# Hybrid decoder block on one core: the first norm's scale by its own transfer, the parameter transposes later, half of group 0 from split parts

## What is computed

```python
u = rms_norm(h, norm1_g)
proj = u @ w_in                      # 1024 x 4608
y_conv = conformer_conv(proj[..., :1024], ...)       # a * sigmoid(g), 31-tap depthwise conv, layer norm, silu, @ w_conv_out
y_attn = attention(q, k, v) @ w_attn_out             # 8 heads of 64, from the next 1536 columns
g = sigmoid(proj[..., 2560:] + b_gates)
h = h + (g[..., :1024] * y_conv + g[..., 1024:] * y_attn) @ w_out
h = h + moe_ffn(rms_norm(h, norm2_g), ...)           # top 4 of 32 experts, clamped SwiGLU, 1024 wide
```

## Time and profile before

| | |
|---|---|
| median of 3 runs | 1130.43 us (1129.95 to 1130.46) |
| the profiled execution | 1127.98 us |
| its span, first to last instruction | 1126.2 us |
| TensorE busy | 967.3 us (86%) |
| VectorE busy | 393.8 us (35%) |
| ScalarE busy | 309.8 us (28%) |
| mean granted clock of TensorE | 0.938 |
| moved by DMA | 432.97 MB, mean 384 GB/s |

### The profile page before, as it was taken

The page is one execution under the profiler, slowest core; times in us unless marked ns, Lnnn a source line. Parts: engine busy times, 40 slices in busy tenths (PEclk is TensorE's granted clock), DMA queues, the critical chain, the costliest instruction groups (busy, mean ns, idle before and its releaser), DMA issues.

```text
span 1126.2 us, 19760 instructions
## 1 busy us (share of the span) xinstructions
PE 967.3 (86%) x7261; PEld 445.8 (40%) x7262; DVE 393.8 (35%) x1014; ACT 309.8 (28%) x534; POOL 5.3 (0%) x27
## 2 busy tenths in 40 slices
PE   6999899998666769899996799998996976998667
PEld 5998689632211213233331233332332321332112
DVE  4699966432111112223232133322322321232111
ACT  4565573222111111212221122221221211222111
POOL 1000000000000000000000000000000000000000
PEclk8999999999888898999998899998999998999887
DMA  7473259999999999999999999999999999999996
GB/s 270 169 290 122 103 182 402 387 414 425 425 427 426 427 428 426 427 425 426 427 427 425 428 425 426 425 428 425 426 425 427 427 426 427 426 427 429 425 427 250
DMA packets 50918, 432.97 MB, mean 384 GB/s; under 512 B 4845, under 2 KB 5265, under 8 KB 18128
## 3 DMA queue, kind: packets, MB, share of 16 engines
q1 hardware_dynamic: 50424, 432.50, 92.3%
q10 hardware_dynamic: 472, 0.16, 0.1%
HBM read 431.59 MB, written 1.05 MB: 384 GB/s over the span
## 4 chain that ended last, share of the span: by engine, by line
PE 48%; DMA 24%; SPq 20%; DVE 4%; issue 2%; ACT 1%; DVEq 0%; ACTq 0%
PE bank L1312 16%; SPq L404 12%; DMA up_odd<-in_w_up_gate 10%; DMA up_even<-in_w_up_gate 10%; PE bank L1043 9%; PE bank L1346 8%; SPq L410 6%; PE bank L1234 5%; DMA down_even<-in_w_down 3%; PE bank L1303 3%; PE bank L1281 2%; DVE up_odd L723 2%; PE bank L1073 1%; PE bank L1332 1%; DVE w_lo L698 1%
## 5 line engine op out<-in xcount | busy, mean ns | idle before, releaser
L1312 PE MATMUL bank<-up_even,reg_r 128*32 128x512 f32 x1472 | 189.9, 661 | 68.2 <-DMA up_even<-in_w_up_gate 68.2
L1312 PE MATMUL bank<-up_odd,reg_r 128*32 128x512 f32 x1408 | 179.4, 654 | 66.1 <-DMA up_odd<-in_w_up_gate 66.1
L998 DVE TENSOR_TENSOR ys<-reg_m,ys 64x512 fp32r<-64x512 f32 x90 | 61.7, 685 | 236.6 <-ACT ys L650 236.0
L1312 PEld LDWEIGHTS bank<-up_even,reg_r 128*32 128x32 f32 x1472 | 47.0, 115 | 203.6 <-DMA up_even<-in_w_up_gate 103.9
L1312 PEld LDWEIGHTS bank<-up_odd,reg_r 128*32 128x32 f32 x1408 | 44.9, 115 | 194.0 <-DMA up_odd<-in_w_up_gate 99.1
L638 ACT ACTIVATE reg_m<-reg_m 128x256 f32<-128x256 f32 x45 | 18.9, 420 | 370.4 <-DVE reg_m L979 370.4
L1234 PE MATMUL bank<-reg_h,reg_r 128*32 128x256 f32 x736 | 93.2, 636 | 0.7 <-DVE reg_r L869 0.7
L979 DVE TENSOR_SCALAR reg_m<-bank 128x256 f32<-128x256 f32 x45 | 19.1, 425 | 211.7 <-PE bank L1312 211.7
L646 ACT ACTIVATE reg_m<-bank,gslot 128x512 f32<-128x512 f32 x45 | 30.9, 688 | 195.5 <-PE bank L1346 195.5
L1346 PE MATMUL bank<-down_even,reg_r 128*32 128x512 f32 x736 | 84.4, 596 | 0.4
L1346 PE MATMUL bank<-down_odd,reg_r 128*32 128x512 f32 x704 | 80.7, 596 | 0.5 <-DMA down_odd<-in_w_down 0.5
(11 more groups left out here) (252 smaller groups left out, 1188.1 us busy)
## 6 DMA issues: line engine op xcount, KB each, us to landing
up_even<-in_w_up_gate SPq DMA_DIRECT2D x64, 2048.0 KB, 35.8
up_odd<-in_w_up_gate SPq DMA_DIRECT2D x64, 2048.0 KB, 38.5
down_even<-in_w_down SPq DMA_DIRECT2D x64, 1024.0 KB, 36.5
down_odd<-in_w_down SPq DMA_DIRECT2D x64, 1024.0 KB, 36.5
down_even<-in_w_in SPq DMA_DIRECT2D x6, 2048.0 KB, 8.4
down_odd<-in_w_in SPq DMA_DIRECT2D x2, 2048.0 KB, 8.7
down_odd<-in_w_in SPq DMA_DIRECT2D x4, 512.0 KB, 8.5
down_odd<-in_w_attn_out SPq DMA_DIRECT2D x1, 2048.0 KB, 8.0
```

Of the source, the lines that this page charges most:

```text
L998: ins = nc.vector.tensor_tensor(ys[64:P, half, :], YR[r, :], ys[0:64, half, :].bitcast(F32), ALU.subtract)
L1312: ins = mm(UP[q * SLOTS:(q + 1) * SLOTS, :], XT[:, k % 2, k // 2 * SLOTS:(k // 2 + 1) * SLOTS], up_columns(a, k, q), start=False, stop=(k ...
```

## The change

The change does four things. `norm1_g` goes by a transfer of its own straight into a new tile `g1c` (128 partitions of 8 values), with its own semaphore `g1_in`; `par` shrinks from 38 to 30 rows, and the multiplies that make uT wait for `g1_in` and not for the parameters. The four parameter transfers of SP are issued behind group 0's, and their transposes on TensorE and copies on VectorE stand later. To fit the order of the scale's transfer, feature p*8+k now lies at partition p, step k: the transposes of x read every eighth column (`features(m)`), and `w_in` is read by `(p k)`, not `(k p)`. Half of group 0 (its columns 256 to 511) is split and computed as the other groups are.

```diff
-        par = sb("par", [P, 38])
+        par = sb("par", [P, 30])
+        g1c = sb("g1c", [P, KD])
...
-        win = w_in.rearrange("(k p) n -> p k n", p=P)
+        win = w_in.rearrange("(p k) n -> p k n", k=KD)
...
SP:
-            sp.dma_start(dwr, conv_dw).then_inc(par_in, 16)
-            sp.dma_start(rows[8:24, :], b_gates...).then_inc(par_in, 16)
-            for r, src in ((36, q_norm_g), (37, k_norm_g)):
-                sp.dma_start(rows[r:r + 1, :]..., src...).then_inc(par_in, 16)
...
                 if i == 0:
                     for c in range(4):
                         sp.dma_start(dst[:, 2 * c:2 * c + 2, :], src[:, 2 * c:2 * c + 2, :]).then_inc(g0_in[c], 16)
+                    sp.dma_start(dwr, conv_dw).then_inc(par_in, 16)
+                    sp.dma_start(rows[0:16, :], b_gates...).then_inc(par_in, 16)
+                    for r, src in ((28, q_norm_g), (29, k_norm_g)):
+                        sp.dma_start(rows[r:r + 1, :]..., src...).then_inc(par_in, 16)
ScalarE:
-            for r, src, n in ((0, norm1_g, 8), (24, conv_dw_b, 4), (28, conv_ln_g, 4), (32, conv_ln_b, 4)):
+            act.dma_start(g1c[:], norm1_g.rearrange("(p k) -> p k", k=KD)).then_inc(g1_in, 16)
+            for r, src, n in ((16, conv_dw_b, 4), (20, conv_ln_g, 4), (24, conv_ln_b, 4)):
                 act.dma_start(rows[r:r + n, :], src.rearrange("(r c) -> r c", c=P)).then_inc(par_in, 16)
...
             def weights_high(i, b):
-                arrived(act, i)
+                if i == 0:
+                    for c in range(4):
+                        act.wait_ge(g0_in[c], 16)
+                else:
+                    arrived(act, i)
...
+            weights_high(0, 1)
             for b in range(2):
                 weights_high(1, b)
VectorE:
-            dve.wait_ge(par_full, 1)
-            nc.vector.tensor_copy(par[:], PAR_BANK[:, 0:38]).then_inc(par_ready, 1)
-            nc.vector.tensor_copy(dwT[:], PAR_BANK[:, 64:...]...).then_inc(par_ready, 1)
             dve.wait_ge(ssx, 1)
             nc.vector.reciprocal(st[:, 4:6], st[:, 2:4]).then_inc(rstd_ready, 1)
-            dve.wait_ge(par_ready, 2)
+            dve.wait_ge(g1_in, 16)
...
-                dve.wait_ge(w_hi_ready, 2 * (i - 1) + b + 1)
+                dve.wait_ge(w_hi_ready, 2 * i + b)
...
-            for i in (1, 2):
-                for b in range(2):
-                    weights_low(i, b)
+            weights_low(0, 1)
+            for b in range(2):
+                weights_low(1, b)
+            dve.wait_ge(par_full, 1)
+            nc.vector.tensor_copy(par[:], PAR_BANK[:, 0:30]).then_inc(par_ready, 1)
+            nc.vector.tensor_copy(dwT[:], PAR_BANK[:, 64:...]...).then_inc(par_ready, 1)
+            for b in range(2):
+                weights_low(2, b)
+            dve.wait_ge(par_ready, 2)
TensorE:
-                        ins = nc.tensor.transpose(bank[...][:, c:c + P], hx[:, m, k * P:(k + 1) * P], ident[:])
+                        ins = nc.tensor.transpose(bank[...][:, c:c + P], features(m)[:, k, :], ident[:])
...
-            pe.wait_ge(par_in, 16 * 9)
-            (the five transposes of rows and dwr, before the rstd products)
...
-            for b in range(2):          # both halves of group 0 in full precision
+            claim(U_G)                  # the first half in full precision, as before
...
+            pe.wait_ge(par_in, 16 * 8)
+            (the five transposes of rows and dwr)
             pe.wait_ge(u_lo_ready, 1)
+            channel_group_bank(0, 1)    # waits for w_lo_ready, then 48 split matmuls
             for b in range(2):
                 channel_group_bank(1, b)
```

More of the change, by code:

```diff
@@ L136, in features @@
             return hx[:, m, :].rearrange("t (f k) -> t k f", k=KD)
-        rows = REG_R[0:38, 512:640]
+        rows = REG_R[0:30, 512:640]
         dwr = REG_R[0:TAPS, 0:512]
@@ L204, in hybrid_block @@
         hotT = sb("hotT", [P, MT, P], F32R)
-        g1c, bgc = par[:, 0:8], par[:, 8:24]
-        dwb, lng, lnb = par[:, 24:28], par[:, 28:32], par[:, 32:36]
-        qg, kg = par[:, 36:37], par[:, 37:38]
+        bgc = par[:, 0:16]
+        dwb, lng, lnb = par[:, 16:20], par[:, 20:24], par[:, 24:28]
+        qg, kg = par[:, 28:29], par[:, 29:30]
         bank = [ctx.enter_context(nc.psum_tensor(f"bank{i}", [P, 512], F32)) for i in range(8)]
@@ L360, in _ @@
                         sp.dma_start(dst[:, 2 * c:2 * c + 2, :], src[:, 2 * c:2 * c + 2, :]).then_inc(g0_in[c], 16)
+                    sp.dma_start(dwr, conv_dw).then_inc(par_in, 16)
+                    sp.dma_start(rows[0:16, :], b_gates.rearrange("(r c) -> r c", c=P)).then_inc(par_in, 16)
+                    for r, src in ((28, q_norm_g), (29, k_norm_g)):
+                        sp.dma_start(rows[r:r + 1, :].rearrange("r (h d) -> r h d", h=2),
+                                     src.rearrange("(r h d) -> r h d", r=1, h=1).to_broadcast([1, 2, HD])).then_inc(par_in, 16)
                 else:
@@ L1024, in _ @@
                         c = k % 2 * T + m * P
-                        ins = nc.tensor.transpose(bank[(U_XT + b) % 4][:, c:c + P], hx[:, m, k * P:(k + 1) * P], ident[:])
+                        ins = nc.tensor.transpose(bank[(U_XT + b) % 4][:, c:c + P], features(m)[:, k, :], ident[:])
                     if m == MT - 1:
                         ins.then_inc(bank_full[(U_XT + b) % 4], 1)
-            pe.wait_ge(par_in, 16 * 9)
[L1029 to L1032, removed]
             pe.wait_ge(rstd_ready, 1)
@@ L1061, in channel_group_bank @@
                         after()
-            for b in range(2):
[L1065 to L1072, removed]
-                        ins = mm(bank[u % 4][:, c * T:(c + 1) * T], stream[0][1][:, k, ch * P:(ch + 1) * P], uT[:, k, :],
-                                 start=(k == 0), stop=(k == KD - 1))
-                ins.then_inc(bank_full[u % 4], 1)
+            claim(U_G)
+            for c in range(2):
+                for k in range(KD):
+                    if c == 0 and k % 2 == 0:
+                        freed(pe, U_XT + k // 2)
+                        pe.wait_ge(g0_in[k // 2], 16)
+                    ins = mm(bank[U_G % 4][:, c * T:(c + 1) * T], stream[0][1][:, k, c * P:(c + 1) * P], uT[:, k, :],
+                             start=(k == 0), stop=(k == KD - 1))
+            ins.then_inc(bank_full[U_G % 4], 1)
+            pe.wait_ge(par_in, 16 * 8)
+            nc.tensor.transpose(PAR_BANK[:, 0:30], rows, ident[0:30, 0:30])
+            for c in range(KC):
+                ins = nc.tensor.transpose(PAR_BANK[:, 64 + c * TAPS:64 + (c + 1) * TAPS], dwr[:, c * P:(c + 1) * P], ident[0:TAPS, 0:TAPS])
+            ins.then_inc(par_full, 1)
             pe.wait_ge(u_lo_ready, 1)
+            channel_group_bank(0, 1)
             for b in range(2):
```

9 lines of the change are left out of this document (3 added, 6 removed).

## The result

| | before | after |
|---|---|---|
| median (4 executions each) | 1130.19 us (1129.80 to 1130.46) | 1122.55 us (1122.02 to 1124.72) |
| the profiled execution | 1127.98 us | 1122.02 us |
| its span | 1126.2 us | 1120.3 us |
| TensorE / VectorE / ScalarE busy | 967.3 / 393.8 / 309.8 us | 969.2 / 395.8 / 311.5 us |

The ratio is 0.9943 with an interval of 0.9922 to 0.9964: 4.1 to 8.8 us faster, and beyond the 0.2% that this measurement can tell from no change. The direction was right, and so was the mechanism. The profiled execution of the kernel before is not one of its four.

A forecast was written before the change was run, and what follows sets the result against it. The bound was when the expert-weight stream gets going, set by TensorE's start of group 1. That start, 4.66 us earlier (29.81 to 25.15), taken from the median 1130.43, gave 1125.7 us; range 1124.6 to 1128.0.

The forecast's parts named there:

- The reciprocal: VectorE's reciprocal of the norm's root mean square, no longer behind parameter copies: at 7.1 to 7.25 us, was 11.29.
- the spread of rstd: TensorE's four rstd matmuls after the transposes of x: start at 7.7 us instead of 11.51, 3.8 us earlier.
- its first half: Group 0's full-precision half on TensorE: 6.8 us at the fast clock, from 10.5 to 17.3.
- the transposes done: Five parameter transposes on TensorE behind group 0's first half: some 0.65 us, over at 17.9.
- the low part: VectorE's low part of group 0's split weights: ready at 19.4 us, after a 1.5 us TensorE stall.
- the taps: The taps on VectorE, behind group 3's second split: start near 41.6 us.
- So 29.81-25.15 = 4.66 us earlier: TensorE's start of group 1: at 25.15 us instead of 29.81, the whole gain of 4.66 us.
- x us of slow clock cost x/2: Rival: group 0's first half starts at the slow clock, keeping 2.4 to 4.3 us of gain; chance 0.12.
- I predict the latter: Choice of base: 1125.7 us from the runs' median 1130.43, not 1123.3 from the profiled execution's 1127.98.
- Moves by the same 4.7: Everything after the taps' start hangs on TensorE and ends 4.7 us earlier, like group 1.
- The gain did not die later: Rival: an unmoved limit, such as the expert stream's start, takes the gain: 1130.4 us, or 1128 for half; chance 0.08.
- W_in in the new row order: Rival: w_in's loads run slower; 30% slower loses the gain, half rate ends at 1142 us; chance 0.05.

The follow-up runs named there:

- e5: The changed kernel with SP's four parameter transfers issued behind group 1's load, their transposes between group 1's halves, copies behind group 2's low parts: 1123.28 us, ratio 0.9956.
- e3: The changed kernel with group 0's second half in full precision again, so without the split half: 1122.59 us, ratio 0.9952 to the kernel before.
- e13: The kernel before with nine extra full-precision 128x128 matmuls that nobody reads, filling two TensorE gaps ahead of group 0: 1124.32 us, ratio 0.9965.
- e12: The kernel before, unchanged, run again beside its own copy on one chip: 1129.60 us, ratio 1.0014.
- e1: The kernel before, unchanged, run for more executions: 1127.61 us, ratio 1.0000.
- e14: The kernel before, unchanged, one execution for one more trace: 1126.41 us.
- e16: The changed kernel, unchanged, one execution for one more trace: 1122.50 us.
- e2: The changed kernel, unchanged, run for more executions: 1121.76 us, ratio 0.9940 to the kernel before.
- e11: The changed kernel, unchanged, run again for its distribution and a third trace: 1122.15 us, ratio 0.9947 to the kernel before.
- e15: The kernel before, unchanged, one execution for one more trace: 1128.78 us.

## Why the prediction was right, and where it failed

**Right: the mechanism and its steps.** The reciprocal at 7.10 (forecast 7.1 to 7.25), the spread of rstd at 7.73 (7.7), group 0's first matmul at 10.30 (10.5, with the shorter rstd matmuls that were left out), its first half 7.14 us (6.8), the transposes done at 17.87 (17.9), the low part at 19.19 (19.4), group 1 at 25.19 (25.15), the taps at 41.65 (41.6). Group 1's transfer landed at 20.9 (20.73); Its place in SP's queue, or what lay ahead of it, kept it from landing sooner: in e5, issued 2.3 us sooner and ahead of the parameters, it landed at 18.38. e3 showed that the split half and the earlier norm are one gain and not two: the limit of group 1's own weights ends both.

**Failed: "So 29.81-25.15 = 4.66 us earlier".** The term that was mis-sized is before's group 0, read from a single execution whose slow stretch was 3.70 us. Over five traces group 1 starts at 29.55 to 30.81, 30.20 in the mean; in after it starts at 25.2 whatever the clock does. The gain at the start is 4.98 us in the mean and up to 5.6, and 0.3 us of the miss. The prediction had the right mechanism for this among its rivals, "x us of slow clock cost x/2", but let it work on the kernel after alone, where a stall covers it. It is before that pays for it, in all five of its traces, and in e13's trace filling the gaps took it away by itself.

**Failed: "I predict the latter".** This is the larger part of the miss. Against the profiled execution the sum gave 1123.3, and that execution came out at 1122.02. The prediction hung the gain on the median of three runs instead. Over all 101 executions of before in these comparisons the mean is 1128.39 (standard deviation 1.89), so that median stood 2.04 above the kernel's own level. Over all 17 of after the mean is 1122.31 (1.03). The difference of the means is 6.08 us, give or take 0.61. The miss against that mean, 1125.77-1122.31 = 3.46 us, is then 2.04 of the base, 0.32 of the start, and 1.10 of what comes later. Why the first four executions of before all lay high is not settled; identical programs came out 2.0 us apart on another chip too (e12). The first comparison alone, 4.1 to 8.8 us, would have allowed a gain of 4.66; all executions together do not. The range's lower end of 1124.6, a gain of 5.8, is worked out nowhere in the prediction, whose sums end at 5.3.

**"Moves by the same 4.7" holds, within what traces can tell.** From group 1's start to the table the two kernels take 192.40 and 192.28 us, from there to the last issue 854.61 and 854.25, and to the end 49.68 and 49.24. The span's means differ by 5.90 us: 4.98 at the start and 0.92 spread over the three later stretches, of which the 0.44 of the last one is e1's tail alone (without it before's mean is 49.03). Each stretch varies by more than that from one execution to the next: the first by whether TensorE's clock fell near 162 to 170 us and again near 211 to 217 us. It is 190.7 long with no fall (e14), 192.0 with the first alone (after's first trace and e16), 192.7 to 192.9 in the four traces of before with both, and 192.5 and 192.6 in e2 and e11, after's two with both. So some 1 us of the gain is left without a cause that is shown.

**The rivals.** The slow clock did eat into the first half, in two of four traces, and cost nothing behind the stall of 1.43 us. The gain did not die later. W_in in the new row order is no slower: group 1 landed at 19.69 to 20.90 in four traces of after, and at 20.46 to 21.17 in five of before. The transposes that read every eighth column cost nothing either: 3.65 us for sixteen against 3.64.

The Trainium skill (TensorE: Matmul & The Clock Gate, Part 4: PE-mode transpose) says that transposes do not engage the full clock. The traces disagree in part: in before's first trace and e1 the granted clock was at 1.00 from 7.75 and 7.47 on, with nothing but the sixteen transposes of x before it; in e12, e14 and e15 the same transposes did not raise it. The prediction's reading, a parameter load of 138 ns as at the fast clock, was right for its trace; the same load took 180 in e12.

The Trainium skill (DMA: Bandwidth & Descriptors, Specifications) puts pieces under 512 bytes below line rate. The scale's 32-byte pieces landed 3.5 us after their issue in after's first trace and were never waited for, so no run here prices that.

## What to carry to other kernels

Before you size a gain, look at more than one execution of the stretch that you remove, and ask how it varies in the old kernel, not only in the new one; hang the gain on as many executions as there are. When a step goes faster, find the next limit and its distance; where two limits meet within 0.2 us, edits that each reach it buy the same microseconds only once, and none that moves one of them alone buys more. A cover (here a stall of 1.4 us) makes the end steady against what lies under it, and that steadiness is part of the gain.

## What the runs showed that was not expected

- Nine products that nobody reads, in two short gaps of TensorE, made the kernel before some 4 us faster by the ratio's middle (0.9965, interval 0.9947 to 0.9983): group 0 went from 15.87 to 16.62 us down to 14.05. About 2.9 us of it stands in the trace at group 1's start.
- The slow stretch at the start of group 0 varied by execution, from about 3.7 to 5.2 us in before and from none to about 3 in after. Sixteen transposes of x had raised the granted clock by 7.8 us in two of before's five traces and not in the other three, and an idle stretch of 2.2 to 2.3 us let it fall again in those two.
- The granted clock's column prints 1.00 ahead of the trace's first entry of the clock (19.55 us in e12), while the matmuls there ran at half the pace. The pace of equal matmuls is what to read there.
- One 2 MB load, issued at the same place of the same program, landed anywhere from 19.69 to 20.90 us in four traces. An edit that seems to move it by 1.3 us in one trace has shown nothing yet.
